# Second layer's modulations as row sums on VectorE inside the first layer's feed-forward

## The reference

```python
s_lat = jax.nn.silu(c)[:, None, :]            # 1024 numbers
s_ctx = jax.nn.silu(c_ctx)                    # 1024 numbers
for li in range(DEPTH_2):                     # 2 layers
    m_lat = jnp.split(s_lat @ w_ada[li] + b_ada[li], 6, axis=-1)   # w_ada[li]: 1024 x 6144
    m_ctx = jnp.split(s_ctx @ w_ada[li] + b_ada[li], 6, axis=-1)
    h = rms_norm_2(x, g_mix[li]) * (1.0 + m_lat[1]) + m_lat[0]
    ...                                       # mixers
    x = x + m_lat[2] * (y @ w_out[li])
    h = rms_norm_2(x, g_ffn[li]) * (1.0 + m_lat[4]) + m_lat[3]
    x = x + m_lat[5] * conv_ffn(h, ffn_up[li], ffn_conv[li], ffn_conv_b[li], ffn_down[li])
    ...                                       # the same for the context in layer 0 alone
```

## Time and profile before

| | |
|---|---|
| median of 3 runs | 2103.53 us (2099.75 to 2104.42) |
| the profiled execution | 2112.82 us, its span 2110.8 us |
| TensorE busy | 2052.6 us (97%) |
| VectorE busy | 1218.9 us (58%) |
| ScalarE busy | 732.7 us (35%) |
| the chain that ended last | TensorE 88%, VectorE 6%, ScalarE 3% |

### The profile page before, as it was taken

One profiled execution on the slowest core, in us unless ns is written; L12 is line 12 of the kernel. 1 busy time (PEld: TensorE's weight loads), 2 busy tenths in 40 slices (PEclk: granted clock), 3 DMA queues, 4 the chain that ended last, 5 costly groups with the idle time before them and its releaser, 6 DMA issues.

```text
span 2110.8 us, 30176 instructions
## 1 busy us (share of the span) xinstructions
PE 2052.6 (97%) x11650; PEld 1644.5 (78%) x11650; DVE 1218.9 (58%) x1954; ACT 732.7 (35%) x1177; POOL 82.6 (4%) x153
## 2 busy tenths in 40 slices
PE   6999999999999989999999999999999899999999
PEld 4666766567788778788888888887788777888887
DVE  4763323467457665576566563446567747667644
ACT  4521112564346444321111122234355533222333
POOL 0001010000031000000000000000130000000000
PEclk9999998899999999999999999999999999999999
DMA  5444355432363301111211112112453022222332
GB/s 189 161 169 171 140 184 186 171 118 80 117 183 99 126 1 39 52 61 60 70 60 60 67 63 69 61 60 68 144 165 132 7 89 71 100 96 93 100 100 80
DMA packets 57090, 214.25 MB, mean 101 GB/s; under 512 B 7248, under 2 KB 7248, under 8 KB 56224
## 3 DMA queue, kind: packets, MB, share of 16 engines
q1 hardware_dynamic: 46752, 168.32, 23.7%
q0 software_dynamic: 8864, 41.71, 6.1%
q10 hardware_dynamic: 1376, 2.85, 0.4%
HBM read 198.69 MB, written 14.16 MB: 101 GB/s over the span
## 4 chain that ended last, share of the span: by engine, by line
PE 88%; DVE 6%; ACT 3%; issue 2%; PEld 1%; ACTq 0%; PEldq 0%; DVEq 0%
PE psum L229 23%; PE psum L230 22%; PE psum L231 22%; PE psum L743 3%; PE psum L517 2%; PE psum L731 2%; PE psum L704 2%; PE psum L1938 2%; PE psum L237 1%; PE psum L2054 1%; PE psum L520 1%; PE psum L1442 1%; PE psum L2460 1%; DVE neg_max L775 1%; PE psum L1468 1%
## 5 line engine op out<-in xcount | busy, mean ns | idle before, releaser
L229 PE MATMUL psum<-h_high,unit_high 128*128 128x512 f32 (+1 forms) x1704 | 621.2, 365 | 0.6 <-DVE unit_low L441 0.6
L230 PE MATMUL psum<-h_low,unit_high 128*128 128x512 f32 (+1 forms) x1704 | 609.5, 358 | 0.0
L231 PE MATMUL psum<-h_high,unit_low 128*128 128x512 f32 (+1 forms) x1704 | 607.3, 356 | 0.0
L433 ACT CAST unit_high<-ring 128x1024 fp32r<-128x1024 f32 x194 | 203.4, 1049 | 575.5 <-PE psum L231 566.0
L229 PEld LDWEIGHTS psum<-h_high,unit_high 128*128 128x128 f32 x1704 | 320.3, 188 | 62.8 <-issue 12.1
L441 DVE TENSOR_TENSOR unit_low<-ring,unit_high 128x1024 fp32r<-128x1024 f32 x194 | 236.9, 1221 | 214.4 <-ACT unit_high L433 214.4
L231 PEld LDWEIGHTS psum<-h_high,unit_low 128*128 128x128 f32 x1704 | 320.1, 188 | 50.8
L230 PEld LDWEIGHTS psum<-h_low,unit_high 128*128 128x128 f32 x1704 | 320.6, 188 | 46.5 <-issue 2.2
L2674 DVE TENSOR_SCALAR conv_out<-psum,parameters 128x512 f32<-128x512 f32 (+1 forms) x132 | 91.2, 718 | 171.2 <-PE psum L231 169.0
L2679 DVE SCALAR_TENSOR_TENSOR conv_out<-psum,parameters,conv_out 128x511 f32<-128x511 f32 (+1 forms) x264 | 166.4, 658 | 22.1 <-DVE conv_out L2674 1.5
L816 ACT ACTIVATE probs<-psum,neg_max 128x768 f32<-128x768 f32 (+4 forms) x136 | 98.7, 728 | 133.6 <-DVE neg_max L775 121.4
(11 more groups left out here) (419 smaller groups left out, 2692.8 us busy)
## 6 DMA issues: line engine op xcount, KB each, us to landing
ring<-in_w_units SPq DMA_DIRECT2D x317, 512.0 KB, 3.4
stacked_heads<-head_parts POOLq DMA_DIRECT2D x48, 192.0 KB, 4.9
x_apart<-xT POOLq DMA_DIRECT2D x1, 3072.0 KB, 11.7
bias<-in_na_bias POOLq DMA_DIRECT2D x2, 1536.0 KB, 8.9
xT<-x_apart POOLq DMA_DIRECT2D x1, 3072.0 KB, 10.2
head_parts<-head_parts_high POOLq DMA_DIRECT2D x6, 384.0 KB, 6.1
head_parts<-p POOLq DMA_DIRECT2D x6, 384.0 KB, 6.0
xT<-in_x ACTq DMA_DIRECT2D x4, 512.0 KB, 6.6
```

The lines of the kernel that those rows point to most:

```text
L229: pe.matmul(out, lh, rh, start=first, stop=False, skip_group_check=True)
L230: pe.matmul(out, lh, rl, start=False, stop=False, skip_group_check=True)
L231: return pe.matmul(out, ll, rh, start=False, stop=last, skip_group_check=True)
L433: act.copy(K.w_high[:, q % 2], K.ring[:, q % RING]).then_inc(K.high_split.sem, 1)
```

## The change

The first layer's modulations stay pairs on TensorE: 24 pairs in passes of 8 and 16. Of the 32 pairs in the dense stage and the recurrence 8 stay, in each group two in the levels (behind levels 2 and 5), one behind the first chunk's apply and one behind the first chunk's advance. The two attentions keep 16. TensorE's drain behind the first pass stands behind the eighth pair, inside the second group.

The second layer's 6144 outputs become 48 units of w_ada transposed: 128 outputs in the partitions, 1024 inputs along the row. They stand in the stream behind units of the first feed-forward: one behind each of the 32 units of turns 1 to 8 of the up products, one behind each of 16 units of the down products. VectorE takes them: the unit times the row of silu(c), the same in all partitions, with the sum of the row as its output (modulate), and for the first 16 units the same once more with silu(c_ctx). The product itself is written over a spare row or over the slot. The rows come by a DMA from c_rows, a new input with c and c_ctx repeated in 128 partitions; ScalarE takes their silu ahead of the up products; a copy goes to DRAM and comes back to another place for the down products. The bias and the gains of layer 1 are added near the end of the down products (finish_layer_modulation). TensorE and ScalarE have their up loop from turn 1 to turn 8, turn 9 written out; VectorE has two loops of four turns.

```diff
-PAIRS_BEHIND = (1, 4, 3, 2, 1, 0)
+PAIRS_BEHIND = (0, 1, 2, 1, 0, 0)
...
-MOD_UNITS = 2 * 6 * KD
-MOD_GROUPS = MOD_UNITS // 4
+MOD_UNITS = 6 * KD
 MOD_PAIRS = MOD_UNITS // 2
-MOD_PASS = (16, 8)
+MOD_PASS = (4, 8)
...
+def modulate(K, dve, rows, i, j, column, streams):
+
+    e, step = place(K, i, j)
+    weights = slot_loaded(K, dve, i, e + 1, step)
+    for s in streams:
+        ins = dve.scalar_tensor_tensor(weights if s == streams[-1] else rows[:, 2], weights, 1.0, rows[:, s], ALU.mult, ALU.mult,
+                                       accum_out=K.mods[:, 1, column, s:s + 1].rearrange("p a b -> p (a b)"))
+    ins.then_inc(K.unit_used.sem, 1)
...
             if j == 3:
                 pe.wait_ge(sig["conditioned"].sem, 1)
-            if j >= 3:
-                modulation_pairs(K, pe, 1)
...
             fill(3)
-            if not b:
-                modulation_pairs(K, pe, 1)
...
             fill(5)
-            modulation_pairs(K, pe, 1)
+            if not b:
+                modulation_pairs(K, pe, 1)
...
             produce(2 * g + 1)
-            modulation_pairs(K, pe, 1)
             fill(KD)
...
                 fill(1)
-                modulation_pairs(K, pe, 1)
+                if lev in (2, 5):
+                    modulation_pairs(K, pe, 1)
...
+def finish_layer_modulation(K, dve):
+
+    for s, units in ((0, 6 * KD), (1, 2 * KD)):
+        ins = dve.tensor_tensor(K.mods[:, 1, 0:units, s], K.mods[:, 1, 0:units, s], prm(K, "b_ada", MOD_UNITS, units), ALU.add)
     link(dve, K.dve_step, ins)
...
+    link(dve, K.dve_step, layer_gains(K, dve, 1))
...
+UP_MODS = range(RING, 9 * RING)
+DOWN_MODS = (*range(1, 9), *range(12, 20))
...
+            @K.block.gpsimd
+            def _(pool):
+                pool.wait_ge(start.sem, start.base + 1)
+                rows_in.up(pool.dma_start(rows_up[:, 0:2], c_rows), 16)
...
+            @K.block.scalar
+            def _(act):
+                act.wait_ge(rows_in.sem, rows_in.n)
+                rows_ready.up(act.activation(rows_up[:, 0:2], rows_up[:, 0:2], ACT.Silu))
...
+                if c_rows is not None and not isinstance(i, int):
+                    modulate(K, dve, rows_up, i, j, ds(i * RING + (j - RING), 1), mod_streams[0])
...
+                dve.wait_ge(rows_ready.sem, rows_ready.n)
+                for j in range(RING):
+                    unit(0, j)
+                for a, b, streams in ((1, 5, (1, 0)), (5, 9, (0,))):
+                    mod_streams[0] = streams
+                    with dve.Fori(a, b) as i:
+                        for j in range(RING):
+                            unit(i, j)
...
+                pool.wait_ge(K.unit_done.sem, K.unit_done.base)
+                pool.wait_ge(rows_out.sem, rows_out.n)
+                rows_in.up(pool.dma_start(rows_down[:, 0:2].rearrange("p n d -> p (n d)"), K.silu_rows), 16)
...
+                if c_rows is not None and j in DOWN_MODS:
+                    if j == 1:
+                        dve.wait_ge(rows_in.sem, rows_in.n)
+                    m = DOWN_MODS.index(j)
+                    at = 4 * KD + m if isinstance(i, int) else i * RING + (4 * KD + m)
+                    modulate(K, dve, rows_down, i, j, ds(at, 1), (0,))
```

More of the change, by code:

```diff
@@ L86, in first_stream @@
         unit(j + 1)
-        if j >= 3:
-            stream.append(("pair", pairs))
-            pairs += 1
     unit(N_STEADY + 1)
@@ L483, in in_turns @@
     elif turns > 2:
-        with eng.Fori(1, turns) as i:
-            for j in range(RING):
-                body(i, j)
+        for a, b in loops or ((1, turns),):
+            if b - a == 1:
+                for j in range(RING):
+                    body(a, j)
+                continue
+            with eng.Fori(a, b) as i:
+                for j in range(RING):
+                    body(i, j)
     for j in range(rest):
@@ L1971, in take_modulations, with layer_gains @@
     return ins
+def layer_gains(K, dve, layer):
+    for n, (name, at) in enumerate((("g_mix", KD), ("g_ffn", 4 * KD))):
+        for s in range(2 - layer * n):
+            ins = dve.scalar_tensor_tensor(K.gains[:, layer, n, s, :], K.mods[:, layer, at:at + KD, s], 1.0,
+                                           prm(K, name, layer * KD, KD), ALU.add, ALU.mult)
+    return ins
 def finish_modulation(K, dve):
@@ L2585, in neighbourhood_attention, with entries, feed_forward @@
     return turn_output
-def feed_forward(K, layer, with_ctx, sums, out):
+UP_MODS = range(RING, 9 * RING)
+DOWN_MODS = (*range(1, 9), *range(12, 20))
+def entries(count, behind):
+    return [n + sum(m < n for m in behind) for n in range(count + RING + 1)]
+def feed_forward(K, layer, with_ctx, sums, out, c_rows=None):
     W = S + C if with_ctx else S
@@ L2600, in feed_forward @@
         hid = arena(K, ctx, "hidden", [P, KF, S + C])
+        with ExitStack() as overlaid:
+            arena(K, overlaid, "below", [P, KD + 3, S + C])
+            rows_down = arena(K, overlaid, "silu_rows", [P, 3, D])
+        rows_up = hid[:, KF - 4:, :].rearrange("p k s -> p (k s)").rearrange("p (n d) -> p n d", d=D)
         inner = ctx.enter_context(ExitStack())
@@ L2635, in unit @@
                 mm.then_inc(K.unit_done.sem, 1)
-            in_turns(pe, 2 * KF, unit, True)
+            in_turns(pe, 2 * KF, unit, True, loops)
         @K.block.scalar
@@ L2872, in feed_forward @@
         low_ready.n += KF
-        used_units(K, KF, more)
+        used_units(K, KF, more, len(DOWN_MODS) if c_rows is not None else 0)
+        K.entries = None
         if gather:
@@ L3064, in second_block @@
         sums = mixers(K, layer, layer == 0, dram, sums, plain if layer == 0 else None)
-        sums = feed_forward(K, layer, layer == 0, sums, dram["out"])
+        sums = feed_forward(K, layer, layer == 0, sums, dram["out"], dram["c_rows"] if layer == 0 else None)
 def mixers(K, layer, ctx_out, dram, sums, plain):
```

109 lines of the change are left out of this document (81 added, 28 removed).

## The result

The changed kernel took 2093.68 us (median of 10 runs, 2084.01 to 2102.53), the kernel before 2104.84 us beside it (10 runs, 2099.75 to 2124.21). The ratio is 0.9942, with a 95% interval of 0.9914 to 0.9971. The forecast was 2092.5 us, 11.0 us under the kernel before, and in the range of 2084 to 2106.

What follows compares the result with a forecast made beforehand. The prediction took TensorE, with work in 97% of the span, as the bound. Its terms -5.4 - 12.0 + 0.3 + 5.9 + 0.2 gave -11.0 us, from the median 2103.5 to 2092.5 us, range 2084 to 2106.

Steps and rivals of the forecast that it cites:

- Dense stage: Ten pairs removed behind dense units 3 to 12 were to save 5.4 of 10.9 us.
- the lost 4.4 us of the seven pairs: Dense stage before 128.45: seven pairs worth 7.6 us save 3.2; the other 4.4 turn into TensorE waits for VectorE.
- The two pairs behind units 10 and 11: Dense stage after 128.45, where VectorE idles: removing these two pairs was to save 2.2 us.
- the pair behind unit 12: End of the dense stage: its removal gives nothing, as the product at 148.68 waits for VectorE's memset.
- Recurrence: Removing 14 of 22 pairs in the recurrence was to save 12.0 of 14 us; the moved drain adds 0.3.
- The drain: TensorE's drain, moved behind the eighth pair inside the second group, lets TensorE run empty: 0.3 us added.
- Up stage: First layer's up products: two row sums of 2.75 us exceed odd units' 2.01 us slack by 0.74, eight times: 5.9 added.
- The even units and turns 5 to 8: Up stage: two row sums fit the even units' 3.22 us slack, one stream's 1.4 us fits both slacks: no waits.
- The silu: ScalarE's silu of 2048 columns and table load, in its 3.13 us idle time before 902.21: 0.2 us added.
- First rival: Up stage: row sum at half rate, 2.44 us, giving 46 us of TensorE waits; 2133 us in all; chance 0.10.
- Second rival: Recurrence without its wide pairs: more stretches fall to 1.2 GHz, six more eat all, about 2103 us; chance 0.10.
- Third rival: All removed pairs at full worth and row sums hidden: -24.9 us, 2078.6 us; chance 0.07.

Runs made afterwards that it cites:

- e3: Changed kernel with three instead of two warming products (big products whose result nobody reads) ahead of the recurrence; 2086.6 us, ratio 0.9933 to the kernel before.
- e8: e4 with a warming product, whose result nobody reads, at each of the attention's 14 missing pair places; 2103.4 us, ratio 0.9982 to the kernel before.
- e6: Changed kernel with both edits, the order of e1 and the third warming product of e3; 2084.0 us, ratio 0.9897 to the kernel before.
- e9: e6 with one more warming product between the recurrence's last products and the attention's first; 2081.9 us, ratio 0.9897 to the kernel before.
- e10: The kernel of e6 measured again, no further edit; 2083.7 us, ratio 0.9897 to the kernel before.
- e2: Changed kernel with both streams' row sums also in turns 5 to 8 of the up stage; 2099.2 us, ratio 0.9972 to the kernel before.
- e4: Changed kernel with the recurrence keeping its 22 pairs and the attention behind it 2 instead of 16; 2104.6 us, ratio 1.0027 to the kernel before.
- e1: Changed kernel with VectorE writing the next low part ahead of the row sums in the up stage; 2087.0 us, ratio 0.9932 to the kernel before.
- e5: The changed kernel measured again, no edit; 2092.4 us, ratio 0.9934 to the kernel before.

## Why the prediction was right, and where it was not

**Dense stage, -5.4 us predicted, -5.9 measured.** Up to L1414 it was -3.2 and is -3.5, and the lost 4.4 us of the seven pairs are there as 4.25 us of new waits for VectorE. The two pairs behind units 10 and 11 gave 2.4 us instead of 2.2. That the pair behind unit 12 gives nothing was right for the time up to the first product. Naming the memset as what is late next was right too, but the step stopped there: it didn't ask what 1.40 us of idle time do to the clock.

**Recurrence, -12.0 and +0.3 predicted.** The levels are 4.88 instead of 5.88 us, as written. As a whole the removal can be read from e3 and e8, which both start the recurrence without a fall, e3 without and e8 with the 14 pairs. Between 159.7 and 318.5 us of before, e3's shift goes from -6.0 to -15.6 and e8's from -6.2 to -4.8, a difference of 11.0 us, with the last of the 14 still to come. The drain shows by itself, behind the eighth pair:

```profile
311.10 0.41 PE L1527 MATMUL psum<-mods_by_row,p 128*128 128x64 f32 x2 [0.32 <-issue]
```

Its 0.32 us of idle time stand behind no other of the eight pairs, and from the pair's last product to the next one it is 0.91 us instead of 0.52: 0.39 us lost, 0.3 forecast.

The forecast had -5.4 - 12.0 + 0.3 = -17.1 us up to the attention's first product. The four kernels with a third warming product (e3, e6, e9, e10) arrive there at -17.3, -17.1, -16.5 and -16.7: where the clock holds, the terms come out as written. The changed kernel's own profile arrives at -8.7: there the clock was at 1.2 GHz for 27 us.

**Up stage, +5.9 predicted, +4.6 measured, by two errors that nearly cancel.** Two row sums take 2.29 us, not 2.75: the read-out hides and no register gap stands ahead of them; it was the lower bound of 2.3 that held. And the slack was not 2.01 us. I had measured it to ScalarE's next cast at 946.64, but TensorE's first weight load for the next unit starts at 946.33 and its first product at 946.44. So the low part, done at 944.63, had 1.70 us to spare. 2.29 - 1.70 = 0.59, near the measured 0.62; the forecast's 0.74 was 2.75 - 2.01. Seven waits instead of eight do the rest. The even units and turns 5 to 8 had none, as predicted, and e2 shows that it is the second sum that decides.

**The silu, +0.2 predicted.** The shift is -24.4 us both at 870 and at 903 us: nothing is lost there.

**First rival, the row sum at half rate: out.** These are the groups of the row sum, by shape:

```profile
L469 DVE SCALAR_TENSOR_TENSOR ring<-ring,hidden 128x1024 f32<-128x1024 f32 x32 | 39.0, 1219 | 0.0
...
L469 DVE SCALAR_TENSOR_TENSOR ring<-ring,silu_rows 128x1024 f32<-128x1024 f32 x16 | 19.5, 1219 | 0.0
L469 DVE SCALAR_TENSOR_TENSOR hidden<-ring,hidden 128x1024 f32<-128x1024 f32 x16 | 19.5, 1217 | 0.0
...
L469 DVE DVE_READ_ACCUMULATOR ring<-ring,hidden x32 | 2.6, 82 | 0.0
```

At 1217 to 1219 ns it is as fast as L1649 in the earlier trace rows, which has no accumulator. By the rule of the Trainium skill ("Vector Engine (DVE) Microarchitecture Reference", Points that are easy to get wrong) it would be twice that; for this shape the trace disagrees.

**Second rival, the clock: half true.** The prediction called itself wrong if the granted clock fell in new places of the recurrence, and it did: a new fall of 10.2 us stands at the recurrence's start, behind the removed pair of unit 12, in four of the six profiles with that wait, and costs 4 us there. What I had not seen is that a wait ahead of the small products would go with it; I had the loss only as a chance of 0.10, and at nothing in the sum. Behind that, the recurrence does not visibly need its pairs: e4 has them and no fewer stretches at 1.2 GHz. The attentions need their own wide work, as e4 and e8 show. At equal clock the change is worth 2089.6 - 2105.4 (to 2106.4) = -15.8 to -16.8 us, and the mean clock of the changed kernel, 0.988 against 0.989 to 0.991, takes some 2 to 6 of it back. So the sum of -11.0 lay close to the measured -11.2 of the medians partly by luck: it left out a loss through the clock and a gain of about the same size. The terms that the traces show (-5.9, about -11.5, +4.6) make -12.8, and some 3 us of the gain at equal clock have no term; the last section has a candidate.

**Third rival, all at full worth: out,** by the waits in the dense stage and in the up stage.

## What to carry to other kernels

Measure a slack to the first thing that needs the result, here the weight load, and queue added work on an engine behind, not ahead of, the piece that another engine waits for: the same row sums cost 4.6 us ahead of the low part and nothing behind it. When work is taken from the bounding engine, ask at each place what idle time it leaves: if wide products stood in a stretch of small ones or covered a wait, look at the granted clock there, and in more than one profile, since the clock may take back what the removal brings and single executions differ in it. And where runs spread by more than the effect, compare the series at equal clock as well, and read the effect from the shift of the same instruction through two traces.

## What the runs showed of the hardware that I had not expected

**The same products run at different periods in different executions, without a wait and at full clock.** In the down stage of the first layer, three 512-column products in a row (high x high, low x high, high x low) take 0.697 to 0.698 us in before, e1, e2 and e6, and 0.686 to 0.687 us in the eight other profiles, worked out from their start times and steady over the stage. It adds up: from 1260 to 1430 us of before, the shift of e6 stays at -17.0, that of the changed kernel goes from -20.1 to -22.2, that of e5 from -15.6 to -19.8. e5 is the changed kernel again, and e10, which goes from -33.6 to -35.7, is e6's kernel: so it belongs to the execution, not to the code. In e5 the up stage gains too, 2.6 us from 1060 to 1240, and e9 gains 9.3 us from 903 to 1434, more than any other. I don't know the cause. It moves a run by 2 to 9 us, and with only one profile of before and one of e2, it may be what the sum at equal clock and e2's extra 2.4 us lack; that is argued, not shown.

**What a wait costs is more than its idle time.** 0.45 us of idle time stood for 0.62 us lost. The weight load waited as well (0.65 us of idle time ahead of the one at 940.11): it starts 0.01 us ahead of its product, where in the kernel before it starts 0.11 ahead (946.33 and 946.44). Over the seven waits 3.6 us of idle time stand for 4.6 us lost.
